# In the recurrent rounds of one mixer, the second direction's mask and state chain change places with a weight's split on VectorE

## The reference

```
def hgrn2_scan(q, k, v, logf, s0, with_output):
    gcum = cumsum(logf within a chunk); g_end = gcum[last]
    k_end = k * exp(g_end - gcum)
    chunk_states = k_end^T v                     # per chunk and head
    s_in = scan: s -> exp(g_end) * s + chunk_states
    att = causal( (q*exp(gcum - g_mid)) (k*exp(g_mid - gcum))^T )
    return att @ v + (q * exp(gcum)) @ s_in
```

## Time and profile before

| | us |
|---|---|
| median of 3 executions | 2481.95 (2480.68 to 2485.22) |
| profiled execution, its own time | 2486.94 |
| its span in the trace | 2485.1 |
| PE busy | 2175.1 (88%) |
| DVE busy | 1712.1 (69%) |
| ACT busy | 1366.1 (55%) |

### The profile page before, as it was taken

How to read it: one execution, slowest core, us unless ns; L and a number is a source line. 1 busy time by engine, 2 the same in 40 slices (tenths; PEclk the granted TensorE clock), 3 DMA queues, 4 the chain that set the end, 5 groups by cost and what they waited for, 6 DMA issues and landing times. The chain is left out here.

```text
span 2485.1 us, 36625 instructions
## 1 busy us (share of the span) xinstructions
PE 2175.1 (88%) x12398; PEld 1790.4 (72%) x12398; DVE 1712.1 (69%) x2903; ACT 1366.1 (55%) x2135; POOL 277.2 (11%) x357
## 2 busy tenths in 40 slices
PE   5999899889998999888886799994889987799993
PEld 4899876589984666667575677783677786577782
DVE  5884626288555698977653699994478674699993
ACT  2663425166453355565333578883476652588882
POOL 0000000000000365555000001101000000001100
PEclk8999999999999999989997799996999887799996
DMA  6455431545543666400121699994221121699991
GB/s 219 162 186 170 142 109 45 203 158 190 175 135 145 250 222 239 162 1 1 43 84 51 230 389 389 390 386 177 94 77 59 52 85 60 219 394 398 393 371 68
DMA packets 127256, 454.99 MB, mean 183 GB/s; under 512 B 13824, under 2 KB 17792, under 8 KB 126976
## 3 DMA queue, kind: packets, MB, share of 16 engines
q1 hardware_dynamic: 116160, 413.14, 45.7%
q0 software_dynamic: 10944, 39.85, 4.2%
HBM read 431.97 MB, written 20.97 MB: 182 GB/s over the span
## 5 line engine op out<-in xcount | busy, mean ns | idle before, releaser
L2722 DVE TENSOR_TENSOR moe_w_lo<-ring,moe_w_hi 128x1024 fp32r<-128x1024 f32 x384 | 462.8, 1222 | 61.9 <-ACT moe_w_hi L2660 57.0
L2660 ACT CAST moe_w_hi<-ring 128x1024 fp32r<-128x1024 f32 x384 | 399.0, 1049 | 147.3 <-PE ps L236 119.4
L373 DVE TENSOR_TENSOR ffn_w_lo<-ring,ffn_w_hi 128x1024 fp32r<-128x1024 f32 x132 | 161.0, 1222 | 101.2 <-ACT ffn_w_hi L325 101.0
L234 PE MATMUL ps<-moe_w_hi,moe_own 128*128 128x512 f32 x512 | 213.8, 418 | 12.1 <-DVE moe_own L2729 11.1
L235 PE MATMUL ps<-moe_w_lo,moe_own 128*128 128x512 f32 x512 | 204.6, 400 | 0.0
L236 PE MATMUL ps<-moe_w_hi,moe_own 128*128 128x512 f32 x512 | 204.6, 400 | 0.0
L325 ACT CAST ffn_w_hi<-ring 128x1024 fp32r<-128x1024 f32 x132 | 137.4, 1044 | 107.4 <-PE ps L236 107.4
L234 PE MATMUL ps<-ffn_h_hi,ffn_w_hi 128*128 128x256 f32 x608 | 173.3, 285 | 11.2 <-DVE ffn_w_lo L373 11.2
L235 PE MATMUL ps<-ffn_h_lo,ffn_w_hi 128*128 128x256 f32 x608 | 172.0, 283 | 0.0
L236 PE MATMUL ps<-ffn_h_hi,ffn_w_lo 128*128 128x256 f32 x608 | 172.0, 283 | 0.0
L234 PE MATMUL ps<-ffn_hid,ffn_w_hi 128*128 128x256 f32 x448 | 131.1, 293 | 12.7 <-DVE ffn_w_lo L373 8.8
(11 more groups left out here) (541 smaller groups left out, 5692.0 us busy)
## 6 DMA issues: line engine op xcount, KB each, us to landing
ring<-in_weights SPq DMA_DIRECT2D x766, 512.0 KB, 5.4
expert_rows<-moe_y POOLq DMA_DIRECT2D x32, 512.0 KB, 7.1
token_rows<-moe_token_rows SPq DMA_DIRECT2D x6, 512.0 KB, 2.6
sq<-in_cmp_w SPq DMA_DIRECT2D x1, 2048.0 KB, 9.8
both<-in_x SPq DMA_DIRECT2D x1, 1024.0 KB, 5.8
both<-in_context SPq DMA_DIRECT2D x1, 1024.0 KB, 8.1
out<-both SPq DMA_DIRECT2D x1, 1024.0 KB, 4.8
cols<-in_cols SPq DMA_DIRECT2D x1, 720.5 KB, 9.1
```

The lines of the kernel that those rows point to most:

```text
L234: pe.matmul(out, w_hi, x_hi, start=start, stop=False)
L373: dve.tensor_tensor(w_lo[:, u % WB], k.ring[:, (first + u) % RING], w_hi[:, u % WB], ALU.subtract).then_inc(w_split, 1)
L2660: act.copy(w_hi[:, j % WB].rearrange("p h f -> p (h f)"), k.slot(act, first + GU + j, e).rearrange("p a f -> p (a f)")).then_inc(w_rounded, 1)
L2722: dve.tensor_tensor(w_lo[:, j % WB].rearrange("p h f -> p (h f)"), k.ring[:, (first + GU + j) % RING].rearrange("p a f -> p (a f)"), w_hi[ ...
```

## The change

In DVE's list of each round, the split of `places[1]` moves from ahead of the mask and chain of head h-2, direction 1, to behind them. Nothing is added or removed, and the lists of the other engines are as they were. In rounds 0, 1 and 10 there is no mask and chain to change places with (in round 10 no split either).

```
@@ -3427,11 +3427,11 @@
                             split(n + WB)
                         if live(h - 1):
                             weigh(h - 1, 0)
-                        for n in places[1]:
-                            split(n + WB)
                         if live(h - 2):
                             mask(h - 2, 1)
                             chain(h - 2, 1)
+                        for n in places[1]:
+                            split(n + WB)
                         if live(h - 1):
                             weigh(h - 1, 1)
                         if h == GH + 1:
```

## The result

The changed kernel takes 2455.05 us (median of 4 executions, 2450.83 to 2458.72) against 2483.59 us of the kernel before (4 executions, 2480.68 to 2486.85). The ratio is 0.9884, with a 95% interval of 0.9862 to 0.9906: 28.5 us or 1.2% faster, and well inside the range. The forecast was 2452.

A forecast was written before the change was run, and what follows sets the result against it. The prediction took DVE's split, waiting for ACT's rounding ahead of chain and mix, as the bound. Gains of 25.2 us (rounds 2 to 7) and 6.3 (round 8) made 31.5, hence 2452 us; range 2446 to 2465, 8 in 10.

The forecast's parts named there:

- What bounded the rounds: Rounds 3 to 7: PE's mix waits 15.6 us for the chain, behind a split that waits 22.3 us for ACT's rounding.
- Rival C: Ahead of the mix, "issue" hides another wait, so nothing changes: 2482 us; chance 0.03.
- DVE's round without the gap: DVE in each of rounds 3 to 7: 22.65 us without waiting, so DVE becomes the bound.
- Rounds 2 to 7: Gain before round 8: 2.3 us in round 2 plus 22.9 in five rounds, together 25.2 us.
- Round 8: Bound by PE, which enters it early and at full clock: 6.3 us gained.
- ACT's loop: ACT's round through PE, from attend 1 through logs_of and back: 22.0 us, 0.65 us to spare, the thinnest margin.
- Rival B: ACT's loop exceeds 22.0 us and becomes the bound, PE idling ahead of carry 0; 1.5 us beyond gives 2456; chance 0.05.
- The clock: PE from mix to last projection: a 3 us gap is mostly followed by a clock drop costing 3.2 us more.
- rival A: Light matmuls of mix and turn, not the gap, lower PE's clock: gain only 16 us, 2467 us; chance 0.08.
- where PE's spare time would stand: PE, needing 21.88 us against DVE's 22.65, waits some 0.8 us per round, expected ahead of the mix.
- From span to time: Profiled execution 2486.94 less 31.5 gives 2455.4 us; the median stands 5.0 lower, so 2452 was taken between 2450.5 and 2455.4.
- Rival D: The moved split comes too late for the next round's second projection: 7 us slower, 2489 us; chance 0.02.

The follow-up runs named there:

- filled gap: Kernel before, with 24 needless 256-column matmuls in PE's gap ahead of each mix of heads 0 to 5; 2468.48 us, ratio 0.9911.
- even rounds: Kernel before, with the new order only in rounds 2, 4, 6 and 8 and the old one in 3, 5, 7 and 9; 2471.28 us, ratio 0.9929.
- rounds 2 to 7: Changed kernel, with the new order kept in rounds 2 to 7 and the old one in 8 and 9; 2455.59 us, ratio 0.9864.

## Why the prediction was right

*What bounded the rounds* was read rightly: "issue" ahead of the mix was the chain, and the chain stood behind ACT's rounding. Removing the wait from either end gives the same rounds. Rival C is out.

*DVE's round without the gap* was to be 22.65 us; it is 22.56, which is what the prediction's eight parts add up to (its 22.65 came from the other way, the round less its idle time). The inner times hold as well: mask 1 was to start at 14.57 and does, chain 1 to end at 18.25 and ends at 18.2, ACT's rounding to end at 15.6 and ends at 15.7. *Rounds 2 to 7* were to gain 25.2: from the round start of round 2 to that of round 8 it was 1995.63 - 1833.75 = 161.88 and is 1964.63 - 1828.24 = 136.39, 25.5 less. *Round 8* was to bring 6.3: from there to the mix of round 9 it was 26.45 (2022.08 - 1995.63) and is 20.44 (1985.07 - 1964.63), 6.0 less. The sum of 31.5 meets 31.5 up to that mix and 31.3 up to the last one. As forecast for one end of the range, the clock fell in round 8's last projection, which took 5.5 us.

*ACT's loop* had enough to spare: it never held PE ahead of `carry` 0 by more than 0.02 us in rounds 3 to 7. Rival B would have needed a loop over 22.56. With VectorE's work cut the round is 22.1, where I had 22.0 for ACT's loop; but that round also runs through chain 0, so no run measured ACT's loop alone.

*The clock* is half of the gain, 15.2 of 31.3 us: 11.1 in rounds 3 to 7 and 4.1 in round 8. The prediction had it as 3.2 us behind most gaps, and in rival A as the gain that would be missing, 12 + 3.2 = 15.2; that the sum is met so closely is luck, as its parts are 0.9 off each way. It also counted three drops behind gaps of about 3 us; in rounds 3 to 7 the clock fell at or behind four of the five, the fourth of 3.62 us. Rival A falls with the filled gap.

*The step that was wrong*, without harm to the sum, is where PE's spare time would stand. I put the 0.8 us ahead of the mix and checked `carry` 1 only as an input of chain 1. But `carry` 1 itself waits for chain 0, which ends 11.4 after the round's start (1908.18), while `attend` 1 ends at 10.9 (1907.71): PE's wait of 0.62 us stands there, and `carry` 1 ended at 1909.46 - 1896.81 = 12.65 instead of 11.9. It cost nothing, because mask 1 comes at 14.57. But it used up more than half of a margin that the prediction had as 1.3 us. ACT's timeline of that round:

```profile
1915.15 0.60 ACT L3241 ACTIVATE h<-ps 128x512 f32<-128x512 f32 x1 [0.72 <-PE ps L236]
...
1918.04 1.52 ACT L3248 ACTIVATE hg_logs<-h,hg_lbs 128x512 f32<-128x512 f32 x2
```

The last projection comes later by PE's wait, ACT's `take` waits 0.72 us for it, and the first logarithm is done at 1918.04 + 0.8 - 1896.81 = 22.0 instead of 21.3, only half a microsecond ahead of the next round's decays at 22.56. In the kernel with more work for VectorE the gap did cost: it grew to 1.64 us, and in two of five rounds the clock fell.

*From span to time.* The spans differ by 2485.1 - 2449.1 = 36.0 us: 5.5 lie ahead of the touched rounds (1833.75 against 1828.24), 31.3 in the stage, and 0.8 are given back behind it. The 5.5 are not of this change: in the five kernels whose instructions up to round 2 are the same (before, changed, filled gap, even rounds, rounds 2 to 7) that start lies between 1828.24 and 1836.41 us. The measured 28.5 with its interval (some 23 to 34) holds the stage's 31.3. The kernel before alone moved by 4 us between its three series (2483.59, 2487.64 and 2487.66). Whether the 3 us between 28.5 and 31.3 are such luck of the executions, or fewer drops of the clock in other executions of the kernel before, stays open; two traces can't tell it. Rival D was not reached: the split could be put another 2.1 us later without harm to the rounds.

## What to carry to other kernels

In an engine's hand-written order, put behind each other by need: work whose input is late and whose result is wanted late (a prefetching split) belongs behind work whose input is there and for which another engine waits. A gap of PE is to be priced with what the clock takes afterwards, here about as much again as a gap of 3 us, in four rounds of five; and the clock's part can make the wait itself longer. And once the wait is gone, look for what each engine's own work per round adds up to: with VectorE at 22.56, the loop of three engines at 22.1 and PE's own 21.9 us, reordering has little more to give in these rounds, as far as these runs show.

## What the runs showed of the hardware that I had not expected

The clock fell not only at or behind gaps of 3 us. It fell with 2.53 us (round 8 of the changed kernel) and 2.58 us (even rounds only), and, with more work for VectorE, in two of five rounds with 1.64 us, where a gap of 0.23 or 0.56 us and light matmuls stood shortly before it; in the other three rounds, with the same 1.64 us and in one of them 0.19 us before it, it did not. Nor did it with 2.99 us at 1882.92 in the kernel before, with 2.52 us in round 8 of the kernel with the split later still, or with 2.93 us in round 8 of the kernel with the new order in even rounds. Gaps of 0.62 us left it at 1.00 in all rounds, and so did the 0.7 to 1.1 us with ScalarE's earlier rounding. So the length of one gap doesn't decide it in these traces; what does, they leave open.
